# A hybrid decoder trunk on one core: x fetched back earlier, two attention tables fetched later, the convolution's LayerNorm finished one projection sooner

## The chip, the cores and the metric

One Trainium2 chip, one core of it, one program. The metric is the device time of one execution in microseconds; a program is timed several times and the median is compared. Everything is float32, with the large products made from three passes over rounded halves (below).

## What is computed

The reference is one inference step of a two-layer trunk on a prompt of 1024 tokens and a sample group of 8 sequences with 4 new tokens each. What matters here is layer 0:

```
proj = h @ e_w_in                      # 512 columns for the convolution, 2304 for q, k, v of 3 groups
glu  = a[:, :256] * sigmoid(a[:, 256:])
a    = silu(layernorm(causal depthwise conv, width 31, of glu))      # 256 channels
for grp, dilation in ((0, 1), (1, 4), (2, 16)):                      # 4 heads of 64 each
    prompt: banded attention over blocks of 128 strided tokens -> o, log sum
    sample: attention of 32 new rows over 8 caches, 129 strided keys per row
attn = mix of the 3 groups' o, weighted by their softmax denominators
x    = x + gate * (concat(a, attn) @ e_w_out)                        # then FFN, layer 1, FFN, final norm
```

## The kernel before

The residual stream `x` lies feature-major in SBUF as 8 tiles of 128 features by 1056 tokens (1024 prompt, 32 sample). `x` does not stay there during layer 0's mixer: it is stored to DRAM (`scratch_x`, 4.2 MB), its place is used by the q and k of two attention groups (`qk_fm`), and it is fetched back in two halves (`x_back`, 2112 KB each) before the down projection adds to it. The prompt attention writes its rows to DRAM as well (`scratch_o`, from the four-slot buffer `o_rows`, by ACT's DMA queue) and the three groups' tables are fetched back as `nat` (1056 KB each, `load_nat`), which are only used at `comb`, after the sample's values.

A weight unit (`w_raw`, 1 MB) is split into a high half by ACT (`split_hi`, L911) and a low half by GpSimd (`split_lo`, L1688). A projection is 16 `part`s: 2 output tiles by 8 input tiles, each 9 matmuls of 352 columns (three passes, three blocks; L1845).

All engines walk one list, `make_plan()`, and each does its share of each item, in that order; semaphores do the rest. So the list is the order on every engine. `mixed(main, fill)` spreads `fill` evenly between the steps of `main`. Attention of one group is 16 steps, each made of four items: `attend_qk` (PE makes scores of two heads, L2048; DVE adds the bias, L1452, and takes the negated maximum into `o_rows`, L1459), `attend_tr` (PE transposes the exponentials, L2056; ACT copies them to `pt`, L1071, and then makes the next step's exponentials, L936), `attend_pv` (PE, L2065; DVE copies to `o_rows`, L1463) and `attend_store` (ACT's queue sends the `o_rows` slot, L1091). The maximum of step i waits until the store of step i-4 has landed.

Small PE results go to two PSUM banks used in turn (`misc`, `misc_slot`); `attend_qk` takes both, so whatever follows it on PE that needs one waits until DVE has added the bias. Large results take two sets of three banks in turn (`big`). From the item `ring` on, during the sample's scores, there are five small banks.

The stages around the change, in order:

- group 1's projections, mixed into attention of group 0, together with 30 of the convolution's 62 taps (`conv`, DVE, L1400);
- group 2's projections v, k, q, mixed into attention of group 1: 12 taps among v's parts, then the LayerNorm's sum (`ln_sum`) early in k, its mean (`ln_mean`) between k and q, and, after q, its variance (`ln_var`);
- attention of group 2, mixed with the sample's keys: `s_kt` transposes a batch's cached keys in five pieces (PE L2086; DVE L1537 and ACT L1132 copy them to `kT`), `s_qk` multiplies them (L2097). SP fetches the keys of batch b+2 (`load_cache`, 1152 KB) when the last piece of batch b has been transposed. `ln_mid` and `sample_load` are among these items.

`ln_mean` is: PE multiplies by a matrix of constants (`mean`, L1900), DVE subtracts (L1484), ACT squares (L1106), DVE adds the squares (L1489). `ln_var` is: PE the same product, ACT Ln (L916) and Exp (L1113), DVE scales two tiles (L1496), ACT Silu on them (L1119), with an activation table load ahead of each.

## Time and profile before

| what | value |
|---|---|
| median of 3 runs | 2721.53 us (2717.16 to 2722.25) |
| the profiled execution, as timed | 2721.19 us |
| its span in the profile | 2719.4 us, 1.8 us less |
| PE busy | 2533.0 us, 93% of the span |
| DVE, ACT, GpSimd busy | 961.0, 571.4, 528.9 us |
| PE, busy share in the stretch 476 to 544 us | between 6 and 7 tenths, the lowest of the span |

The time of the profiled execution and the median differ by 0.34 us. PE is the engine to watch: where it is idle, the row's bracket says how long and what ended the idle time.

### The profile page before, as it was taken

To read this page: it belongs to the slowest core of one execution; us is meant where nothing else is said; L and a number is where in the kernel's file an instruction comes from. 1 tells how busy PE (TensorE), PEld (TensorE's weight loads), DVE (VectorE), ACT (ScalarE), POOL (GpSimd) and SP (SyncE) were. 2 spreads that over 40 slices of the span, in tenths; PEclk is the share of its full clock that TensorE was granted. 3 is DMA by queue.
4 is the path that set the end of the run, shared out by engine and by line. 5 is a ranking of instruction groups with operands and counts; after the bars stand their busy time and mean duration, and the time that the engine had idled before them with its cause. 6 is when DMAs were issued, how large, how long until landed. Compare 5 with 4: busy or idle time off the path is not lost.

```text
span 2719.4 us, 35656 instructions
## 1 busy us (share of the span) xinstructions
PE 2533.0 (93%) x16005; PEld 2411.7 (89%) x16005; DVE 961.0 (35%) x1556; ACT 571.4 (21%) x722; POOL 528.9 (19%) x175
## 2 busy tenths in 40 slices
PE   7798889688899999999999799997999999999996
PEld 4797778457899999999999799997999999999996
DVE  3465653346422222122224522436422222222226
ACT  3312223422411111111112311032311111111112
POOL 1321001100322211222112423111422211122220
PEclk8899999788999999999999899999999999999998
DMA  8112242563112221122212388310011111111101
GB/s 308 58 59 88 86 130 87 199 207 105 47 63 78 78 93 63 63 94 78 77 64 77 118 284 289 112 56 32 32 47 47 47 47 39 40 47 47 47 32 64
DMA packets 163522, 246.66 MB, mean 91 GB/s; under 512 B 5870, under 2 KB 150676, under 8 KB 162218
## 3 DMA queue, kind: packets, MB, share of 16 engines
q1 hardware_dynamic: 151078, 179.41, 20.1%
q0 software_dynamic: 3872, 60.82, 6.5%
q10 hardware_dynamic: 8420, 4.15, 0.5%
q8 instruction: 126, 2.06, 0.3%
q14 instruction: 26, 0.21, 0.0%
HBM read 225.69 MB, written 62.52 MB: 106 GB/s over the span
## 4 chain that ended last, share of the span: by engine, by line
PE 74%; DVE 3%; DMA 2%; issue 1%; ACT 1%; SPq 0%; DVEq 0%; ACTq 0%
PE ps L1845 67%; PE ps L1882 2%; PE ps L1956 1%; PE ps L1900 1%; DVE nt L1345 1%; DMA scratch_o<-o_rows 1%; DMA cache<-in_cache_b_kv 1%; DMA w_raw<-in_e_w_out 0%; PE ps L2097 0%; DVE h_lo L1371 0%; DVE nt L1354 0%; DVE tmp L1196 0%; PE ps L2086 0%; PE ps L1964 0%; DVE ln_t L1475 0%
## 5 line engine op out<-in xcount | busy, mean ns | idle before, releaser
L1688 POOL TENSOR_TENSOR w_lo<-w_raw,w_hi 128x2048 fp32r<-128x2048 f32 x93 | 435.5, 4683 | 1789.0 <-ACT w_hi L911 1789.0
L1845 PE MATMUL ps<-h_hi,w_hi 128*128 128x352 f32 x3024 | 667.8, 329 | 6.1 <-DVE h_lo L1213 3.4
L1845 PE MATMUL ps<-h_hi,w_lo 128*128 128x352 f32 x3024 | 653.6, 324 | 0.0
L1845 PE MATMUL ps<-h_lo,w_hi 128*128 128x352 f32 x3024 | 653.4, 324 | 0.0
L1845 PEld LDWEIGHTS ps<-h_hi,w_hi 128*128 128x128 f32 x3024 | 511.7, 190 | 27.0 <-issue 22.4
L1845 PEld LDWEIGHTS ps<-h_hi,w_lo 128*128 128x128 f32 x3024 | 520.7, 188 | 0.0
L1845 PEld LDWEIGHTS ps<-h_lo,w_hi 128*128 128x128 f32 x3024 | 516.2, 189 | 0.0
L1206 DVE SCALAR_TENSOR_TENSOR x<-ps,mod,x 128x704 f32<-128x704 f32 x448 | 315.5, 746 | 317.0 <-PE ps L1845 317.0
L1253 DVE TENSOR_TENSOR tmp<-ps,tmp 128x1056 f32<-128x1056 f32 x44 | 55.3, 1257 | 729.7 <-PE ps L1845 729.7
L911 ACT ACTIVATE w_hi<-w_raw 128x2048 fp32r<-128x2048 f32 x93 | 177.7, 1911 | 503.9 <-PE ps L1845 400.4
L1845 PE MATMUL ps<-mid_hi,w_hi 128*128 128x352 f32 x1248 | 274.6, 328 | 8.5 <-DVE acc_s L1207 5.2
L1845 PE MATMUL ps<-mid_hi,w_lo 128*128 128x352 f32 x1248 | 271.1, 325 | 0.0
L1845 PE MATMUL ps<-mid_lo,w_hi 128*128 128x352 f32 x1248 | 270.8, 325 | 0.0
L1845 PEld LDWEIGHTS ps<-mid_hi,w_hi 128*128 128x128 f32 x1248 | 214.3, 191 | 15.2 <-issue 6.3
L1845 PEld LDWEIGHTS ps<-mid_hi,w_lo 128*128 128x128 f32 x1248 | 216.3, 189 | 0.0
L1845 PEld LDWEIGHTS ps<-mid_lo,w_hi 128*128 128x128 f32 x1248 | 213.9, 189 | 0.0
L916 ACT ACTIVATE tmp<-ps 128x1056 f32<-128x1056 f32 x52 | 54.4, 1052 | 464.6 <-PE ps L1845 435.7
L952 ACT ACTIVATE mid_hi<-tmp 128x1056 fp32r<-128x1056 f32 x44 | 47.9, 1088 | 427.7 <-DVE tmp L1253 427.7
L1317 DVE TENSOR_TENSOR mod<-ps,vecs 128x18 f32<-128x18 f32 x48 | 8.2, 171 | 238.3 <-PE ps L1964 237.8
L1400 DVE SCALAR_TENSOR_TENSOR conv_a<-ext_p,vecs,conv_a 128x1024 f32<-128x1024 f32 x60 | 84.7, 1412 | 0.0
L1882 PE MATMUL ps<-h_hi,w_hi 128*128 128x352 f32 x192 | 43.1, 368 | 31.6 <-ACT h_hi L1028 31.6
L1882 PEld LDWEIGHTS ps<-h_hi,w_hi 128*128 128x128 f32 x192 | 37.6, 223 | 35.6 <-issue 35.6
(260 smaller groups left out, 1705.0 us busy)
## 6 DMA issues: line engine op xcount, KB each, us to landing
w_raw<-in_ada_w SPq DMA_DIRECT2D x48, 1024.0 KB, 6.6
w_raw<-in_ffn_w_gate_up SPq DMA_DIRECT2D x44, 1024.0 KB, 5.1
out_kv_sample<-in_cache_b_kv POOLq DMA_DIRECT2D x8, 4088.0 KB, 19.3
w_raw<-in_ffn_w_down SPq DMA_DIRECT2D x22, 1024.0 KB, 5.0
cache<-in_cache_b_kv SPq DMA_DIRECT2D x28, 512.0 KB, 6.2
w_raw<-in_e_w_in SPq DMA_DIRECT2D x11, 1024.0 KB, 5.7
w_raw<-in_o_w_in SPq DMA_DIRECT2D x10, 1024.0 KB, 10.2
out_kv_sample<-in_cache_b_kv POOLq DMA_DIRECT2D x8, 1016.0 KB, 6.4
```

The source lines that it names most:

```text
L911: act.activation(w_hi[u % 2], w_raw[r.slot], ACT.Copy).then_inc(w_hi_done, 1)
L916: return act.activation(blocks(dst), big(t)[:, :, 0:BLK], func, **kw).then_inc(big_free[t % 2], 1)
L952: act.activation(mid_hi[:, it.j % 2, m, :], tmp[:, m, :], ACT.Copy).then_inc(hid_hi, 1)
L1206: dve.scalar_tensor_tensor(dst, src, g, dst, ALU.mult, ALU.add)
L1253: dve.tensor_tensor(blocks(tmp[:, m, :]), T[:, :, 0:BLK], blocks(tmp[:, m, :]), ALU.mult)\
L1345: dve.scalar_tensor_tensor(nt[:, k, 0:SEQ], x[:, k, 0:SEQ], mod[:, c, k, 0:1], rs[:, 0:SEQ], ALU.mult, ALU.mult).then_inc(xn_made, 1)
L1400: ins = dve.scalar_tensor_tensor(dst, src, w, dst, ALU.mult, ALU.add)
L1688: pool.tensor_tensor(w_lo[raw_of[u].slot], w_raw[raw_of[u].slot], w_hi[u % 2].bitcast(F32), ALU.subtract)\
L1845: mm = pe.matmul(big(t)[:, b, 0:BLK], wt, xt[:, k, b * BLK:b * BLK + BLK], start=(k == 0 and n == 0), stop=(k == K - 1 and n == 2))
L1882: mm = pe.matmul(big(t + m)[:, b, 0:BLK], halves[s][:, k, m * P:m * P + P], xt[:, k, b * BLK:b * BLK + BLK], start=(k == 0 and step == 0), ...
L1900: mm = pe.matmul(big(t)[:, b, 0:BLK], mean_w, src[:, b * BLK:b * BLK + BLK], start=True, stop=True)
L1956: mm = pe.matmul(misc(it.misc)[j:j + S_TOK, 0:256], cs[:, k, :], w[:, k, :], start=(k < 4), stop=(k >= 4), skip_group_check=True)
```

## The change

Four moves in the list, and the waits that go with them; the work itself is the same.

1. Four more convolution taps (34 instead of 30) are mixed into attention of group 0; the last eight are among the first ten parts of group 2's v, with the request for group 2's bias table (`bias_in`) behind them and `ln_sum` three parts later.
2. `ln_mean` moves from between k and q to between v and k; `ln_var` from behind q to between k and q.
3. The first fetch of `x` (`x_back`, k=1) moves from the middle of group 2's attention to its beginning, and GpSimd waits with it until the keys of batch 1 have landed (`keys_landed(1)`).
4. The tables of groups 0 and 1 (`nat`) are no longer fetched at `sample_in` but when the keys of batch 2 and of batch 3 have landed.

```diff
-    mixed(attention(0), among(among(v + k + q, taps[20:50]), [ada] * 8))
+    mixed(attention(0), among(among(v + k + q, taps[20:54]), [ada] * 8))
...
-    k = k[:2] + [one("bias_in", g=2), norm_a[0]] + k[2:]
-    mixed(attention(1), among(among(v, taps[50:62]) + k + [norm_a[1]] + q, [ada] * 8))
+    v = among(v[:10], taps[54:62]) + [one("bias_in", g=2)] + v[10:13] + [norm_a[0]] + v[13:]
+    mixed(attention(1), among(v + [norm_a[1]] + k + [norm_a[2]] + q, [ada] * 8))
     ada_out()
-    norm_a[2]()
     last = attention(2)
     mixed(last[:3], [])
     items.append(Item("sample_in"))
+    items.append(Item("x_back", k=1))
+    items.append(Item("nat_in", g=0, b=2))
...
-    half = (len(last) - 3) // 2
-    mixed(last[3:15] + [one("ln_mid"), one("sample_load")] + last[15:3 + half] + [one("x_back", k=1)] + last[3 + half:], sample)
+    mixed(last[3:15] + [one("ln_mid"), one("sample_load"), one("nat_in", g=1, b=3)] + last[15:], sample)
...
+            def keys_landed(b):
+
+                slot, turn = cache_at(b)
+                pool.wait_ge(cache_loaded[slot], 48 * turn)
...
-                    load_nat(0)
-                    load_nat(1)
                 elif it.kind == "nat_in":
 
-                    pool.wait_ge(big_ready, score_item.big + 1)
-                    load_nat(2)
+                    if it.g < 2:
+                        keys_landed(it.b)
+                    else:
+                        pool.wait_ge(big_ready, score_item.big + 1)
+                    load_nat(it.g)
                 elif it.kind == "x_back":
                     if it.k:
+                        keys_landed(1)
                         pool.wait_ge(sc_max, 32)
```

On PE, at the boundary between v and k of group 2, the changed kernel has this (`tmp` is what is averaged, `sc` the exponentials; the changed kernel's lines are 7 higher, L1907 is `mean`):

```order
L1907 MATMUL ps<-tmp,mean_w 128x352 x3
L2055 MATMUL ps<-qk_fm_99 128x256 x2
L1852 MATMUL ps<-h_hi,w_hi_61 128x352 x3
L1852 MATMUL ps<-h_lo,w_hi_61 128x352 x3
L1852 MATMUL ps<-h_hi,w_lo_59 128x352 x3
L2063 MATMUL ps<-ident_sb,sc 128x128 x4
```

Before, the same stretch began with the scores: the product with `mean_w` is new there, and on DVE `ln_mean`'s two subtractions and its addition now stand ahead of the bias for these scores.

```order
L1484 SCALAR_TENSOR_TENSOR conv_a<-ps,conv_a 128x1056 x2
L1489 TENSOR_TENSOR tmp<-tmp 128x1056
L1452 TENSOR_TENSOR sc<-ps,bias 128x256 x2
L1459 TENSOR_REDUCE o_rows<-sc 128x2
L1463 COPY o_rows<-ps 128x128
```

On ACT, at the boundary between k and q, the changed kernel has `ln_var` ahead of a step's copy to `pt` and the next exponentials; before, a copy to `pt` of the same step stood there with `ln_mean`'s squares, and these rows up to the Silu came behind q:

```order
L916 ACT_TABLE_LOAD
L916 ACTIVATE tmp<-ps,vecs 128x1056
L1113 ACT_TABLE_LOAD
L1113 ACTIVATE tmp<-tmp 128x1056
L1119 ACT_TABLE_LOAD
L1119 ACTIVATE tmp<-conv_a,vecs 128x1056 x2
L1071 ACTIVATE pt<-ps 128x512
L936 ACT_TABLE_LOAD
L936 ACTIVATE sc,o_rows<-sc,o_rows 128x128 x2
```

On GpSimd's queue, at the beginning of group 2's attention (`cache_loaded0` and `cache_loaded1` are the keys' landings; L1815 is the fetch of `x`, L1713 that of a table), the changed kernel has:

```order
L1797 DMA select<-in_select 128x32
L1815 DMA x<-scratch_x 128x4224 [waits misc_free0,x_stored,sc_max,cache_loaded1]
L1713 DMA nat<-scratch_o 128x8x264 [waits o_stored2,o_stored1,o_stored3,o_stored0,cache_loaded0]
L1820 DMA kv_s<-scratch_kv 32x3x256 [waits kv_stored,mixed_ready]
L1821 DMA bias_s<-scratch_bias_s 128x480
L1713 DMA nat<-scratch_o 128x8x264 [waits o_stored2,o_stored1,o_stored3,o_stored0,cache_loaded1]
L1815 DMA x<-scratch_x 128x4224 [waits x_stored,k_stored,sc_max]
```

Before, both tables stood right behind `select`, without a wait for keys, and both fetches of `x` behind `bias_s`. SP's order is the same in both kernels.

## Rows read from the trace of the kernel before

**Rows 1.** The page: the chain that ended last, shares by engine.

```profile
PE 74%; DVE 3%; DMA 2%; issue 1%; ACT 1%; SPq 0%; DVEq 0%; ACTq 0%
```

**Rows 2.** Windows: us, busy (count) of PE, PEld, DVE, ACT, POOL, PEclk, DMA share, GB/s.

```profile
444.00:488.00 44.00, 40.36 (x281) 35.67 (x279) 10.52 (x23) 15.75 (x41) 6.55 (x2) 1.00 0.20 62
488.00:502.00 14.00, 3.59 (x19) 2.47 (x19) 7.78 (x37) 11.02 (x17) 3.47 (x5) 0.66 1.03 362
...
527.00:535.00 8.00, 1.53 (x11) 0.99 (x8) 0.74 (x2) 0.67 (x2) 0.00 (x0) 0.68 1.00 387
```

**Rows 3.** Waits of PE, 488 to 535 us: us in total, times, longest.

```profile
PE ps L2048 <- DVE sc L1452: 6.5, 1, 6.5
PE ps L2086 <- DMA cache<-in_cache_b_kv: 6.1, 1, 6.1
PE ps L2056 <- ACT sc L936: 3.4, 1, 3.4
```

**Rows 4.** Timeline behind q: start, us, engine, line, tiles, [idle before <-releaser].

```profile
486.12 2.02 PE L1900 MATMUL ps<-tmp,mean_w 128*128 128x352 f32 x6
...
488.07 0.49 PE L2048 MATMUL ps<-qk_fm 64*128 64x128 f32 x4
...
488.51 1.14 ACT L916 ACTIVATE tmp<-ps,vecs 128x1056 f32<-128x1056 f32 x1
...
492.07 2.43 DVE L1496 TENSOR_TENSOR conv_a<-conv_a,tmp 128x1056 f32<-128x1056 f32 x2 [5.60 <-ACT tmp L1113]
...
494.54 2.42 ACT L1119 ACTIVATE tmp<-conv_a,vecs 128x1056 f32<-128x1056 f32 x2 [1.20 <-DVE conv_a L1496]
...
496.98 1.28 ACT L936 ACT_TABLE_LOAD   x1
498.28 0.40 ACT L936 ACTIVATE sc<-sc,o_rows 128x128 f32<-128x128 f32 x1
...
500.46 0.80 PE L2048 MATMUL ps<-qk_fm 64*128 64x128 f32 x4 [0.56 <-ACT pt L1071]
```

**Rows 5.** Timeline, a bias addition at 426 us and the stretch of `ln_mean`.

```profile
426.08 0.42 DVE L1452 TENSOR_TENSOR sc<-ps,bias 128x256 f32<-128x256 f32 x1 [1.64 <-PE ps L2048]
...
442.88 1.94 PE L1900 MATMUL ps<-tmp,mean_w 128*128 128x352 f32 x6
...
449.41 1.26 DVE L1489 TENSOR_TENSOR tmp<-tmp 128x1056 f32<-128x1056 f32 x1 [2.13 <-ACT tmp L1106]
...
451.14 0.49 PE L2048 MATMUL ps<-qk_fm 64*128 64x128 f32 x4 [1.07 <-DVE o_rows L1463]
...
452.43 0.73 PE L1845 MATMUL ps<-h_hi,w_hi 128*128 128x352 f32 x3
```

**Rows 6.** DMA: volume, 488 to 506 us; one issue, 489.5 to 491.6 us.

```profile
DMA packets 4942, 6.51 MB, mean 362 GB/s; under 512 B 228, under 2 KB 4395, under 8 KB 4941
...
cache<-in_cache_b_kv SPq DMA_DIRECT2D x1, 512.0 KB, 11.4
```

**Rows 7.** DMA issues, 507 to 509.7 us: KB each, median us to landing.

```profile
scratch_o<-o_rows ACTq DMA_DIRECT2D x2, 33.0 KB, 2.8
```

**Rows 8.** DMA issues, 520.5 to 522.5 and 523.5 to 525 us.

```profile
x<-scratch_x POOLq DMA_DIRECT2D x1, 2112.0 KB, 12.0
...
scratch_o<-o_rows ACTq DMA_DIRECT2D x2, 33.0 KB, 9.1
```

**Rows 9.** DMA issues, 551 to 553 us.

```profile
scratch_o<-o_rows ACTq DMA_DIRECT2D x2, 33.0 KB, 4.6
```

**Rows 10.** Timeline of DVE: the maximum of steps 4, 7, 8 and 15 of group 2.

```profile
511.66 0.42 DVE L1459 TENSOR_REDUCE o_rows<-sc 128x2 f32<-128x256 f32 x1
...
534.26 0.42 DVE L1459 TENSOR_REDUCE o_rows<-sc 128x2 f32<-128x256 f32 x1 [8.18 <-DMA scratch_o<-o_rows]
...
539.05 0.42 DVE L1459 TENSOR_REDUCE o_rows<-sc 128x2 f32<-128x256 f32 x1 [0.44 <-issue]
...
570.77 0.42 DVE L1459 TENSOR_REDUCE o_rows<-sc 128x2 f32<-128x256 f32 x1
```

## Prediction

> **What bounds the kernel now.** The page's chain comes first: three quarters of it is PE's own work [rows 1], so a change that alters no work can only give back, or add, stretches in which PE stands idle or runs slowly. The list of waits then says where these lie. In the 47 us from 488 to 535 us there are three: 6.5 us for DVE's bias addition and 3.4 us for ACT's exponentials, both at the beginning of group 2's attention, and 6.1 us for a cache of keys [rows 3]. The windows show what goes with them: the granted clock is 0.66 and 0.68 there, that is partly at the lower of the two levels, 1.2 GHz, after PE had been idle, and the DMA engines are full, 1.03 and 1.00 [rows 2]. What the lower level costs a form is in two rows: the same scores take 0.49 us at 488.07 and 0.80 us at 500.46 [rows 4].
>
> The timeline shows why the first two waits exist. `ln_var`'s product ends at 488.14, ACT makes Ln and Exp, DVE scales, ACT makes the Silu until 496.96, loads a table and reaches the exponentials at 498.28 [rows 4]; attention waits behind all that on DVE and on ACT. The third has a companion: at 534.26 DVE's maximum of step 7 had waited 8.18 us for a store of `o_rows` [rows 10], whose landing took 9.1 us where it takes 2.8 without company [rows 7, 8]. The fetch of `x`, issued in the same two microseconds, took 12.0 [rows 8]. So the real chain of this stage is the store that must land before the maximum four steps on.
>
> **The change, part by part.** I count from T, the start of a `mean` product.
>
> *`ln_mean` between v and k.* Before, the addition of squares ends at 449.41 + 1.26 = 450.67, which is T + 7.8 for T = 442.88 [rows 5]. Now the scores of step 7 come right behind the product, take both small PSUM banks, and their bias addition is queued on DVE behind that addition: the first bank is free at T + 7.8 + 0.4 = T + 8.2 [rows 5]. PE has until then the product (1.5 until the next matmul can start, an estimate from its 1.94), the scores (0.7) and one part: about 1.5, since before, PE needed 451.14 - 1.07 - 442.88 = 7.2 us for a product, three parts and one `attend_pv` [rows 5]. That is 3.7. It then stands for 4.5 us at the transposes. With the product itself, this boundary costs **6.0 us**.
>
> *`ln_var` between k and q.* From the start of Ln to the end of the Silu it took 496.96 - 488.51 = 8.45 us [rows 4]. ACT copies `pt` only behind it, at about T + 10.9, and the item `tokens_new` wants that bank; PE has 7.2 + 0.4 us of work until then, so it stands 3.3 us. Then `tokens_new`, its copy off (0.7, an estimate), and the step's scores put the next part at T + 12.3, against 452.43 - 442.88 = 9.55 before, with 0.4 of transposes changing sides [rows 5]: **+2.3 us**. What is queued behind: step 12's exponentials, which have a table load of 1.28 more ahead, and the high half of a weight unit on ACT; both have a step's length to spare.
>
> At this place a page of the Trainium skill counts more: "ScalarE: Activation LUTs", section "What ACT_TABLE_LOAD costs", puts a switch at the load plus a drain of 1.38 us, 2.66 us in all. Here 496.98 + 1.28 = 498.26 and the exponential starts at 498.28 [rows 4], so there is no drain in this trace; by the page, with three switches until the Silu, the stall would be some 4 us longer and the sum 4 us later. I go by the rows.
>
> *Clock.* Two new idle stretches, 4.5 and 3.3 us, in a stage that ran at the full level, 1.00 from 444 to 488 us [rows 2]. The old ones of 9.8 and 6.1 us were followed by the lower level [rows 2, 3]. If one of 5 to 7 us of lower level follows each, at 0.80 against 0.49 per form, they cost 2 us or more each; if none, nothing. I take 2.5 together. The stage up to the end of q gets 6.0 + 2.3 + 2.5 = **10.8 us** longer; bounds 8.3 and 14.
>
> *Taps.* Four more in the earlier stage and four fewer in the later: the same DVE work, hidden behind parts of PE in both. I take 0, with 1 us either way.
>
> *Behind q.* From here I count in the old times, as if q ended at the same moment. The two waits of 6.5 and 3.4 go, and so does the product. But step 2's scores cannot be at once: the first cache must land and `q_own` be filled, for which DVE needs GpSimd's memset first. I expect them at 491.6, 8.9 before 500.46 [rows 4]. The pace behind is (570.77 - 539.05) / 7 = 4.53 us a step [rows 10], so step 4's maximum would be at 491.6 + 9.1 + 1.3 = 502.0 instead of 511.66.
>
> That is the first maximum that needs a store, and here the moved fetch of `x` counts. From 488 to 506 us 6.51 MB are moved, at 362 GB/s [rows 6]; 2.16 MB of these are the two tables, which leave, and 2.16 MB of `x` come in their place. The last piece of batch 1's keys took 11.4 us [rows 6] and landed at 500.5; without the tables' share I expect it at 494 to 495. `x` is issued then and takes up to 12.0 us [rows 8], so the engines are full until about 507, and the store of step 0, issued near 499, lands with it: 8 us, as in rows 8. Step 4's maximum comes at 507 instead of 502.0. The gain there is **4.7 us**, half of what the waits in rows 3 promise.
>
> *From step 4 to step 8.* Before: 539.05 - 511.66 = 27.4 us [rows 10]. Undisturbed: 4 x 4.53 = 18.1. `x` is gone from here, but the two tables are now fetched here, each when a cache has landed. Each is 1.06 MB, 2.9 us at the rate of rows 6. A store that meets one is late by between 1.8 (4.6 - 2.8, beside a cache load [rows 7, 9]) and 6.3 (9.1 - 2.8 [rows 7, 8]) if the maximum waits for it, by nothing otherwise. I take 2.5 each, near the lower row since a table is half of `x`. So 23.1 us, **4.3 less**. Sum of this stage -9.0; bounds: -19.0 with no store hit at all, -1.4 with both tables at 6.3.
>
> Behind step 8 nothing differs: the second half of `x`, the third table and the value caches start by the same events.
>
> **Sum.** +10.8 - 9.0 = +1.8 us on the profiled 2721.19, and 0.34 between that execution and the median: 2723.3.
>
> **The rivals.** 0.2% of the time, 5.4 us, is what a measurement here can tell from no change.
>
> *Faster.* `x` disturbs the early stores little, because step 0's store goes out before `x` is at full rate (step 4's maximum at 504, -7.7), and each table costs 1 us (-7.3); idle stretches in q's stage bring almost no lower clock (+8.8). Together -6.2: 2715.3. For it speaks that the two visible waits, 9.8 and 6.1 us [rows 3], go for sure; against it that 6.0 us at the v and k boundary follow from the order alone.
>
> *Slower.* The tables take `x`'s place as the transfer that holds the stores in the middle of the stage: both hit a store that a maximum waits for, at the 6.3 us of rows 7 and 8. The stage then gives back 1.4 only: +9.4, 2730.9. It decides from about 4.3 us for each table on. For it speaks that the maximum waits for the store that is just issued, so any transfer finds one; against it that a table is half as large as `x`. The Trainium skill says, in "DMA: Bandwidth & Descriptors", section "Queues, rings and completion order", that each DMA engine takes turns between its queues, packet by packet; by that rule a small store is slowed by how many queues are busy beside it, however much they hold, and a table would delay it as `x` does. Rows 8 and 9 leave this open, since the 4.6 us had one other queue busy and the 9.1 us two.
>
> *Nothing.* Both sides are small: no lower clock, q's stage hides most of `ln_mean` after all, and the stage behind gains little: 2721.5.
>
> **How the numbers follow.** The forecast of near cancelling has 0.46, with a range of its own of 2718 to 2728; faster 0.29, slower 0.19, nothing 0.06. From the faster case nearly all, and a little of the forecast's lower edge, lies below 2716.1: 0.29. Above 2727.0 lie most of the slower case and the forecast's upper edge: 0.23. Within: 0.48. The range 2713 to 2731 reaches to both rivals' times and leaves out what the bounds allow beyond them.
>
> **What would show it.** PE waits of about 4.5 us at the transposes behind `ln_mean` (for DVE's bias addition) and of about 3.3 us at `tokens_new` behind `ln_var` (for ACT's copy to `pt`); the clock below 1 behind them; step 4's maximum waiting for a store until the fetch of `x` has landed; no wait above 3 us for the keys of batch 3. I am wrong if PE does not wait behind `ln_mean`, if the early stores land within 5 us beside `x`, or if a store beside a table takes 8 us or more.

## The result, and the profile after

The changed kernel takes 2725.61 us in the median of 20 runs (2721.07 to 2730.98); the kernel before took 2719.04 in 20 runs beside them, 2.5 less than in the three runs that the forecast started from. The ratio is 1.0027, 95% interval 1.0020 to 1.0033, that is 7.3 us more (5.4 to 9.0). The forecast was 2723.3 with a range to 2731.0, on the side of no change; the loss is just over the bound of 0.2%. The profiled execution took 2728.81 us, 3.2 over the median, with a span of 2727.1, 7.7 us over the span before.

The chain's shares answer [rows 1]: PE's share is higher, and DMA's too, since the chain now goes through the stores of `o_rows`.

```profile
PE 77%; DVE 4%; DMA 3%; ACT 1%; issue 1%; SPq 0%; ACTq 0%; DVEq 0%
```

The windows answer [rows 2]; q now ends near 502 us, so the beginning of group 2's attention is the third row here. The stage that ran at full clock before, 444 to 488 us, is at 0.92 now.

```profile
444.00:488.00 44.00, 38.47 (x251) 33.10 (x250) 12.88 (x30) 20.48 (x40) 4.56 (x1) 0.92 0.24 79
488.00:502.00 14.00, 13.77 (x107) 12.86 (x105) 1.05 (x4) 3.84 (x11) 0.00 (x0) 1.00 0.07 20
502.00:516.00 14.00, 10.52 (x62) 8.10 (x63) 8.30 (x43) 6.64 (x25) 4.25 (x4) 0.67 0.91 298
516.00:530.00 14.00, 6.88 (x52) 3.72 (x45) 2.52 (x8) 2.90 (x8) 0.37 (x1) 0.74 0.82 281
```

The timeline of the changed kernel has the two idle stretches of PE that the order promised. At the boundary of v and k it is the wait for DVE's bias addition, 4.18 us, with the same parts of k taking 1.08 us a row behind it where they took 0.65 ahead of it; at the boundary of k and q it is the wait for ACT's copy to `pt`, 3.47, then 0.93 for DVE. These rows answer [rows 5] and [rows 4].

```profile
403.70 1.94 PE L1907 MATMUL ps<-tmp,mean_w 128*128 128x352 f32 x6
...
406.79 0.64 PE L1852 MATMUL ps<-h_lo,w_hi 128*128 128x352 f32 x3
407.27 0.64 PE L1852 MATMUL ps<-h_hi,w_lo 128*128 128x352 f32 x3
412.08 1.09 PE L2063 MATMUL ps<-ident_sb,sc 128*128 128x128 f32 x4 [4.18 <-DVE sc L1452]
412.82 1.23 PE L1852 MATMUL ps<-h_hi,w_hi 128*128 128x352 f32 x3
413.85 1.08 PE L1852 MATMUL ps<-h_lo,w_hi 128*128 128x352 f32 x3
...
465.72 0.36 PE L2035 MATMUL ps<-ident_sb,k_new 128*32 128x128 f32 x1 [3.47 <-ACT pt L1071]
...
467.65 0.80 PE L2055 MATMUL ps<-qk_fm 64*128 64x128 f32 x4 [0.93 <-DVE kv_rows L1437]
468.38 1.25 PE L1852 MATMUL ps<-h_hi,w_hi 128*128 128x352 f32 x3
```

Windows of PE alone (us, busy and count, granted clock, DMA share, GB/s) say how long the lower of the two levels, 1.2 instead of 2.4 GHz, stays behind the first of these stretches: from shortly before 412 to 418 us. Behind the second stretch it stays from 465.8 to 472.6.

```profile
408.00:410.00 2.00, 0.00 (x0) 1.00 0.11 36
410.00:412.00 2.00, 0.00 (x0) 0.79 0.00 0
412.00:414.00 2.00, 1.92 (x8) 0.50 0.04 8
414.00:416.00 2.00, 2.00 (x9) 0.50 0.00 0
416.00:418.00 2.00, 2.00 (x9) 0.51 0.00 0
418.00:420.00 2.00, 1.93 (x26) 1.00 0.00 0
```

That length is not fixed. The kernel with the LayerNorm part alone, below, has the same items here and the same wait of 4.2 us, and there the lower level lasts 3.4 us in all:

```profile
408.00:410.00 2.00, 2.00 (x9) 0.52 0.03 8
410.00:412.00 2.00, 2.00 (x10) 0.63 0.00 0
412.00:414.00 2.00, 1.93 (x25) 1.00 0.00 0
```

So it is with the tables first and with the taps early; with x in the middle it is 6.8 us as here. Behind the second stretch all five have 6.8 or 6.9 us.

Behind q, the timeline of GpSimd's queue and DVE's maxima in group 2 answer [rows 8] and [rows 10]. `x` is issued at 512.31 and takes 14.4 us; the store that the maximum of step 4 waits for goes out in two pieces, 2.2 and 2.8 us later (514.51 and 515.09), and lands with it. The three fences are the timeline, the DMA issues from 511 to 514 us, and the chain (start and length).

```profile
512.31 0.53 POOL L1815 DMA_DIRECT2D x<-scratch_x  x1 [6.48 <-DMA cache<-in_cache_b_kv]
...
527.03 0.42 DVE L1459 TENSOR_REDUCE o_rows<-sc 128x2 f32<-128x256 f32 x1 [8.24 <-DMA scratch_o<-o_rows]
...
540.78 0.42 DVE L1459 TENSOR_REDUCE o_rows<-sc 128x2 f32<-128x256 f32 x1 [3.09 <-DMA scratch_o<-o_rows]
...
551.49 0.42 DVE L1459 TENSOR_REDUCE o_rows<-sc 128x2 f32<-128x256 f32 x1 [3.69 <-DMA scratch_o<-o_rows]
```

```profile
x<-scratch_x POOLq DMA_DIRECT2D x1, 2112.0 KB, 14.4
```

```profile
515.09 11.82 DMA scratch_o<-o_rows
```

For the whole way I take marks from the timelines: the start of DVE's maximum (L1459 here) of a step, written group,step; the first product with `mean_w` behind the down projection (675.66 before, 683.05 after); and the end of the span. In us:

| stretch | before | changed | difference |
|---|---|---|---|
| start to 1,0 | 357.30 | 354.63 | -2.7 |
| 1,0 to 1,6 (v; taps) | 40.38 | 44.32 | +3.9 |
| 1,6 to 1,15 (both LayerNorm places) | 71.69 | 87.63 | +15.9 |
| 1,15 to 2,4 | 42.29 | 40.45 | -1.8 |
| 2,4 to 2,8 | 27.39 | 24.46 | -2.9 |
| 2,8 to 2,15 | 31.72 | 34.71 | +3.0 |
| 2,15 to the norm | 104.89 | 96.85 | -8.0 |
| norm to end | 2043.74 | 2044.05 | +0.3 |

The sum is +7.7, the difference of the spans. Of the first row, 1.9 us lie ahead of group 0's first maximum (211.75 before, 209.9 changed), where the two lists are the same. The marks stand a little differently to the parts of q in kernels with another number of items between the steps, so they are good to a microsecond or two, and one execution is not its median: four profiles with the same items from 1,0 to 1,15 have 129.0, 129.1, 130.7 and 131.95 us there.

### The profile page after: what moved, and what is told of

It is laid out like the page before. It is cut to its first block, busy times and chain, and to the rows that moved or that the text cites. A ratio compares the mean times of both kernels' runs of the same rounds, so it can differ in the third digit from the quotient of the medians.

```text
span 2727.1 us, 35657 instructions
## 1 busy us (share of the span) xinstructions
PE 2533.8 (93%) x16005; PEld 2413.0 (88%) x16005; DVE 960.9 (35%) x1556; ACT 571.7 (21%) x722; POOL 528.5 (19%) x175
## 4 chain that ended last, share of the span: by engine, by line
PE 77%; DVE 4%; DMA 3%; ACT 1%; issue 1%; SPq 0%; ACTq 0%; DVEq 0%
PE ps L1852 69%; PE ps L1889 2%; DMA scratch_o<-o_rows 2%; PE ps L1963 1%; PE ps L1907 1%; DVE nt L1345 1%; DMA cache<-in_cache_b_kv 1%; DMA w_raw<-in_e_w_out 0%; PE ps L1971 0%; PE ps L2104 0%; PE ps L2072 0%; DVE h_lo L1371 0%; PE ps L2055 0%; DVE nt L1354 0%; DVE tmp L1196 0%
```

## The experiments

Twelve kernels, each timed 5 to 12 times beside the kernel before; ratios are to those runs, and differences in us are these ratios times their median.

| kernel | median | before beside it | ratio, 95% interval |
|---|---|---|---|
| LayerNorm part alone | 2724.38 | 2719.53 | 1.0016, 1.0007 to 1.0025 |
| fetches alone | 2717.09 | 2719.53 | 0.9991, 0.9982 to 1.0001 |
| both products behind transposes | 2718.47 | 2719.53 | 0.9998, 0.9989 to 1.0006 |
| x in the middle | 2731.44 | 2719.53 | 1.0038, 1.0026 to 1.0051 |
| PE kept busy | 2722.70 | 2718.45 | 1.0015, 1.0004 to 1.0027 |
| taps early | 2727.77 | 2718.45 | 1.0030, 1.0019 to 1.0040 |
| tables first | 2724.66 | 2718.45 | 1.0026, 1.0011 to 1.0042 |
| behind transposes, old fetches | 2718.71 | 2718.45 | 1.0004, 0.9994 to 1.0013 |
| taps alone | 2710.65 | 2719.48 | 0.9973, 0.9961 to 0.9984 |
| taps and fetches | 2709.72 | 2719.48 | 0.9958, 0.9944 to 0.9971 |
| mean behind the scores | 2724.45 | 2717.77 | 1.0021, 1.0012 to 1.0030 |
| that, variance behind transposes, old fetches | 2719.67 | 2717.77 | 1.0010, 1.0001 to 1.0019 |

**The LayerNorm part alone.** The changed kernel's list up to q, with the fetches of before, also on GpSimd's side:

```diff
     items.append(Item("sample_in"))
-    items.append(Item("x_back", k=1))
-    items.append(Item("nat_in", g=0, b=2))
...
-    mixed(last[3:15] + [one("ln_mid"), one("sample_load"), one("nat_in", g=1, b=3)] + last[15:], sample)
+    half = (len(last) - 3) // 2
+    mixed(last[3:15] + [one("ln_mid"), one("sample_load")] + last[15:3 + half] + [one("x_back", k=1)] + last[3 + half:], sample)
...
+                    load_nat(0)
+                    load_nat(1)
...
-                        keys_landed(1)
```

> The kernel before with the first two moves alone (taps, bias request, LayerNorm steps); the fetches of x and of the two tables stand as before. Both theories: the last maximum of group 1 ends its attention 16 to 17 us later than before (469.37 to about 486), with PE idle 4.2 us at the transposes behind ln_mean and 3.5 us at tokens_new behind ln_var, each followed by about 6.7 us at a granted clock of 0.50. Theory A (these idle stretches and the half clock behind them are the loss, and the fetches change little): before + 4 to + 11 us, that is within 4 us of the changed kernel. Theory B (the LayerNorm's cost is given back behind q and the moved fetches are the loss): within 3 us of before.

Measured: 4.4 us slower than before (1.9 to 6.8), with PE waits of 4.2 and 3.5 us in the same places and 129.1 us from 1,0 to 1,15 (112.1 before, 131.95 changed). The lower clock behind the first wait lasted half as long as I expected, 3.4 us. So the greater part of the loss is there without any moved fetch. What it shows beside that: 1,15 to 2,4 took 35.3 us, 7.0 less than before and 5.1 less than in the changed kernel. The gain behind q that I forecast is there, as long as `x` is not.

**The fetches alone.** The LayerNorm and tap lines of before, the fetches of the changed kernel.

```diff
-    mixed(attention(0), among(among(v + k + q, taps[20:54]), [ada] * 8))
+    mixed(attention(0), among(among(v + k + q, taps[20:50]), [ada] * 8))
...
-    v = among(v[:10], taps[54:62]) + [one("bias_in", g=2)] + v[10:13] + [norm_a[0]] + v[13:]
-    mixed(attention(1), among(v + [norm_a[1]] + k + [norm_a[2]] + q, [ada] * 8))
+    k = k[:2] + [one("bias_in", g=2), norm_a[0]] + k[2:]
+    mixed(attention(1), among(among(v, taps[50:62]) + k + [norm_a[1]] + q, [ada] * 8))
     ada_out()
+    norm_a[2]()
```

> The kernel before with the last two moves alone: x fetched behind the keys of batch 1, the two tables behind the keys of batches 2 and 3; taps and LayerNorm as before. Both: group 1's last maximum stays at 469.4 within 1 us, and the waits of 6.5 and 3.4 us at the beginning of group 2's attention stay. Theory A: the time is that of before within 4 us, since behind q the stage swaps one transfer for another of the same size. Theory B (the moved fetches are the loss): before + 5 us or more, with a maximum of group 2 that waits 6 us or more for a store.

Measured: 2.4 us faster, which the interval does not tell from nothing (-4.9 to +0.3); 112.5 us from 1,0 to 1,15 and 42.8 to 2,4. Theory B, that the fetches are the loss, falls. (The profiled execution, 2711.79 us, is the fastest of the eleven, 5.3 under their median.) The timeline shows why an early `x` does no harm here: it is issued at 496.48 and takes 12.4 us, to 508.9. The store of step 0, which must land before step 4's maximum, goes out at 507.15, when `x` is nearly in, and lands in 2.0 us (timeline; DMA issues from 507 to 508.3 us).

```profile
496.48 0.54 POOL L1816 DMA_DIRECT2D x<-scratch_x  x1 [6.98 <-DMA cache<-in_cache_b_kv]
...
507.15 0.54 ACTq L1092 DMA_DIRECT2D scratch_o<-o_rows  x1
```

```profile
scratch_o<-o_rows ACTq DMA_DIRECT2D x2, 33.0 KB, 2.0
```

With the LayerNorm behind q the store goes out 10.7 us behind `x`; with the LayerNorm early, 2.2.

**Both products behind the transposes.** The list is cut at the two boundaries, so that each product comes behind the transposes of a step (`main[24]` and `main[44]` are the `attend_pv` behind them).

```diff
-    mixed(attention(1), among(v + [norm_a[1]] + k + [norm_a[2]] + q, [ada] * 8))
+    main = attention(1)
+    fill = among(v + [norm_a[1]] + k + [norm_a[2]] + q, [ada] * 8)
+    at = [fill.index(norm_a[1]), fill.index(norm_a[2])]
+    mixed(main[:24], fill[:at[0]])
+    norm_a[1]()
+    mixed(main[24:44], fill[at[0] + 1:at[1]])
+    norm_a[2]()
+    mixed(main[44:], fill[at[1] + 1:])
```

> The changed kernel, with ln_mean and ln_var each a few items further on, behind a step's transposes instead of behind its scores; the boundaries of v, k and q move with them. Theory A: no PE wait above 1.5 us at either place (4.2 and 3.5 before this edit), the granted clock stays at 1.00 there, and group 1's last maximum comes at 472 within 2 instead of 486.6. The kernel as a whole gains 8 to 14 us on the changed one. Rival (the part behind q is set by transfers, not by when q ends; a shorter stage is given back there): the stage gains as much, the whole under 5 us.

Measured: as fast as before (-3.0 to +1.6 us), 7.8 us under the changed kernel by the ratios. From 1,0 to 1,15 it took 121.9 us, 10 less than changed; one part of q, about 1.5 us, now comes behind the last mark and not ahead of it. PE's longest wait at the first place is 1.5 us (of the waits from 385 to 430 us, in total, times, longest):

```profile
PE ps L2062 <- DVE o_rows L1470: 1.5, 1, 1.5
```

The clock did not stay at 1.00 throughout: 0.80 from 402 to 408 us, 0.91 to 414.

The long waits are gone, but most of their time is not. From 1,0 to 1,15 (windows, length less PE's busy time) PE idles 17.2 us here, 19.9 in the changed kernel and 10.6 before; what fell is its busy time, from 112.0 to 104.6 us, with the clock at 0.96 where it was 0.91. The cut list puts every item between the steps at another place, and the idle time now lies in many waits of 2.1 us or less.

**x in the middle.** The changed kernel with `x_back` (k=1) where it stood before.

```diff
-    items.append(Item("x_back", k=1))
...
-    mixed(last[3:15] + [one("ln_mid"), one("sample_load"), one("nat_in", g=1, b=3)] + last[15:], sample)
+    half = (len(last) - 3) // 2
+    mixed(last[3:15] + [one("ln_mid"), one("sample_load"), one("nat_in", g=1, b=3)] + last[15:3 + half] + [one("x_back", k=1)] + last[3 + half:], sample)
```

> The changed kernel with the first fetch of x back in the middle of group 2's attention; tables late and LayerNorm early as changed. Theory A (x holds up the store of step 0, which took 11.8 us beside it): the first store waited for lands in 6 us or less, the maximum of step 4 comes 4 us or more sooner than 40.5 us behind group 1's last, and a store in the middle is late by 6 us in its place: the whole within 3 us of the changed kernel. Rival (the caches and the k and v stores beside it hold the store up, with or without x): the maximum of step 4 does not move by more than 1.5 us.

Measured: 1,15 to 2,4 in 32.9 us, 7.6 less than changed: `x` it was that held step 4, and the rival (caches and k and v stores alone) falls. But `x` now goes out at 530.81, 0.9 us behind the second table, and step 8's maximum pays for it; a store there took 10.55 us in the chain. 2,4 to 2,15 took 67.6 us against 59.2, and the whole is 10.3 us slower than before (7.1 to 13.9), at the upper edge of what was expected or over it. The profiled execution, 2722.96 us, is the fastest of the six and 8.5 under their median, so the trace does not hold all of that loss.

```profile
513.83 0.42 DVE L1459 TENSOR_REDUCE o_rows<-sc 128x2 f32<-128x256 f32 x1 [0.76 <-DMA scratch_o<-o_rows]
...
529.93 0.89 POOL L1713 DMA_DIRECT2D nat<-scratch_o  x1 [6.24 <-DMA cache<-in_cache_b_kv]
530.81 0.56 POOL L1815 DMA_DIRECT2D x<-scratch_x  x1
...
543.13 0.42 DVE L1459 TENSOR_REDUCE o_rows<-sc 128x2 f32<-128x256 f32 x1 [8.25 <-DMA scratch_o<-o_rows]
```

**PE kept busy.** Work whose result is overwritten fills the two idle stretches: 27 matmuls at the first part of k, 18 at that of q. Nothing is left out.

```diff
+                if m == 0 and k == 0:
+                    big_slot(it.big)
+                    for i in range({("k", 2): 9, ("q", 2): 6}.get((it.role, it.g), 0)):
+                        for b in range(3):
+                            pe.matmul(big(it.big)[:, b, 0:BLK], halves[0][:, 0, 0:P], h_hi[:, 0, b * BLK:b * BLK + BLK],
+                                      start=True, stop=True)
                 dense_tile(it.big + m, KT, lambda s, k: halves[s][:, k, m * P:m * P + P], h_hi, h_lo, k)
```

> The changed kernel with repeated work put into the two idle stretches: at the first part of group 2's k, 27 matmuls (high half by high half of that part) are made and overwritten before the part itself, and 18 at the first part of q, some 4.4 and 2.9 us of PE's time in waits of 4.2 and 3.5 us. The results are the same. Theory A (an idle stretch costs its own length and about as much again as 3.3 us in the 6.7 us at half clock behind it): the granted clock stays at 1.00 in both places, the first parts behind take 1.45 us again, not 2.6, and group 1's attention, from its first maximum to its last, takes 5 to 7 us less than the 131.95 of the changed kernel. Rival (the half clock does not come from the idle stretch, but by the run or the place): the clock falls all the same, and the stage is as long or longer.

Measured: the clock stays at 1.00 in all windows of both places, and 1,0 to 1,15 takes 126.4 us instead of 131.95, as Theory A expected, although PE does more. The transposes come without a wait, and the parts behind them are at full speed:

```profile
403.66 4.59 PE L1874 MATMUL ps<-h_hi,w_hi 128*128 128x352 f32 x27
408.09 0.64 PE L1852 MATMUL ps<-h_hi,w_hi 128*128 128x352 f32 x3
...
409.55 0.63 PE L2069 MATMUL ps<-ident_sb,sc 128*128 128x128 f32 x4
409.93 0.73 PE L1852 MATMUL ps<-h_hi,w_hi 128*128 128x352 f32 x3
410.50 0.65 PE L1852 MATMUL ps<-h_lo,w_hi 128*128 128x352 f32 x3
```

```profile
406.00:412.00 6.00, 6.00 (x41) 5.88 (x40) 2.70 (x4) 3.44 (x8) 0.00 (x0) 1.00 0.00 0
412.00:418.00 6.00, 5.25 (x46) 4.33 (x45) 1.38 (x5) 1.98 (x2) 4.25 (x1) 1.00 0.29 83
```

So the lower clock behind the two stretches cost up to 5.6 us in the changed kernel. Counted from 1,6, since the filling stands behind it, it is 82.4 us against 87.6; three other profiles with the same items have 86.3 to 87.1. The price is thus 4.0 to 5.3 us. The whole: 4.1 us over before (1.1 to 7.3), against 7.3; the direction fits, the two intervals overlap.

**Taps early.** The last eight taps also go into group 0's stage; empty items keep everything else in place.

```diff
-    mixed(attention(0), among(among(v + k + q, taps[20:54]), [ada] * 8))
+    mixed(attention(0), among(among(v + k + q, taps[20:62]), [ada] * 8))
...
-    v = among(v[:10], taps[54:62]) + [one("bias_in", g=2)] + v[10:13] + [norm_a[0]] + v[13:]
+    v = among(v[:10], [lambda: None] * 8) + [one("bias_in", g=2)] + v[10:13] + [norm_a[0]] + v[13:]
```

> The changed kernel with its last eight convolution taps moved too, from among group 2's v into attention of group 0 (42 taps there); everything else keeps its place. Theory A (eight taps among ten parts hold up the scores of steps 3 to 6, 3 us by the trace): the way from group 1's first maximum to that of step 6 takes 40.4 within 1 us as in the kernel before, not 44.3, and attention of group 0 gets longer by under 1 us: the whole 3 us under the changed kernel. Rival (the vector engine is as full in group 0's stage): group 0's stage gets longer by 2 to 4 us and nothing is won.

Measured: both halves of both theories. 1,0 to 1,6 takes 38.4 us instead of 44.3, so the eight taps did hold up those steps, by 4.2 to 5.9 us against the four profiles that have them at the same places (42.6 to 44.3). But group 0's attention, from its first maximum to its last, takes 131.5 us (125.6 changed), with a PE wait of 6.5 us there, and the whole is 8.2 us over before (5.2 to 10.9). In this profile 42 taps there cost more than they save, and the rival is right too.

```profile
PE ps L2028 <- DVE sc L1452: 6.5, 1, 6.5
```

**Tables first.** The changed kernel, with the tables of groups 0 and 1 at the beginning again.

```diff
-    items.append(Item("nat_in", g=0, b=2))
...
-    mixed(last[3:15] + [one("ln_mid"), one("sample_load"), one("nat_in", g=1, b=3)] + last[15:], sample)
+    mixed(last[3:15] + [one("ln_mid"), one("sample_load")] + last[15:], sample)
...
+                    load_nat(0)
+                    load_nat(1)
                 elif it.kind == "nat_in":
...
```

> The changed kernel with the tables of groups 0 and 1 fetched at the beginning again, as before, but x still behind the keys of batch 1. Theory A (what holds the stores is whatever large transfer is under way, so the order only moves the loss): 4.3 MB stand together at the beginning, the maximum of step 4 comes 40 to 45 us behind group 1's last (40.5 with the tables late), and step 4 to step 15 takes 53 to 56 us (59.2 with them late): the whole within 3 us of the changed kernel. Rival (a late table costs a store at every place where it meets one, an early one nothing): the whole 4 us or more under the changed kernel.

Measured: 38.9 us from 1,15 to 2,4 and 55.6 from there to 2,15 (40.5 and 59.2 in the changed kernel), as expected except that step 4 lost nothing by the tables; 7.1 us over before (3.0 to 11.4), so the same as the changed kernel as far as twelve runs between 2716 and 2737 us can tell. The rival, 4 us or more under the changed kernel, is not borne out, but the interval just reaches it.

**Behind the transposes, old fetches.** The cut list of the third run with the fetches of the first; no further edit.

> The LayerNorm steps behind the transposes, as in the run of that name, with all fetches as before. Theory A (with q ending without idle stretches, the early x costs step 4 some 7 us, as the kernel with the LayerNorm part alone showed: 35.3 us from group 1's last maximum to step 4's, and not 40.5): 33 to 36 us here, against 41.3 with x early, the maximum of step 15 at 94 to 96 us behind group 1's last against 99.5, and the whole 3 to 6 us under the 2718.5 of that run, so under both kernels. Rival (the values' stage is set by transfers that start at fixed places and gives any gain back): step 15 earlier by as much, the whole within 2 us of 2718.5.

Measured: 37.6 us to 2,4 (41.3 with `x` early) and 96.8 to 2,15 (99.5), about half of the gain that I expected; the whole, 1.1 us over before (-1.6 to +3.5), is not under that run. Here the rival is the nearer one. PE idles 17.2 us from 1,0 to 1,15 here too.

**Taps alone, taps and fetches.** After eight kernels one thing stood out: with 34 taps, group 0's attention took 119.8 to 122.4 us in six profiles (125.6 in that of the changed kernel), with 30 taps 125.7 and 126.0. So the tap move was tried by itself, and with the fetches.

```diff
-    mixed(attention(0), among(among(v + k + q, taps[20:50]), [ada] * 8))
+    mixed(attention(0), among(among(v + k + q, taps[20:54]), [ada] * 8))
...
-    mixed(attention(1), among(among(v, taps[50:62]) + k + [norm_a[1]] + q, [ada] * 8))
+    mixed(attention(1), among(among(v, taps[54:62]) + k + [norm_a[1]] + q, [ada] * 8))
```

> The kernel before with one thing changed: 34 convolution taps in attention of group 0 instead of 30, and 8 instead of 12 among group 2's v. LayerNorm and fetches as before. Theory (with 34 taps in this arrangement five of six kernels ran attention of group 0, first to last maximum, in 119.8 to 122.4 us at a granted clock of 0.99, against 125.7 and 126.0 with 30 taps at 0.93; the idle stretches there stay too short or too scattered for the clock to fall): 120 to 123 us here, with group 1's stage at 112 within 1.5, and the whole 3 to 6 us under before. Rival (the granted clock there falls or not by chance, whatever the taps): 125 us or more in this profile, or the whole within 2 us of before.

> The same with the moved fetches too (x behind the keys of batch 1, the two tables behind those of batches 2 and 3); only the LayerNorm stays as before. Theory: the gains add, 3 to 6 us from the taps and 2.4 from the fetches, so 5 to 8 us under before, the fastest version of this study. Rival (a gain ahead of the values' stage is given back there): within 2 us of the kernel with the moved fetches alone, 2.4 us under before.

Measured: taps alone are 7.3 us faster than before (4.4 to 10.6), taps and fetches 11.4 (7.9 to 15.2), the fastest kernel here and faster than both that were compared. In the profile of the taps alone, group 0's attention took 122.3 us, 3.8 less, and group 1's 110.0, 2.1 less. In that of taps and fetches group 0's took 126.5, so the size of that part is not firm: over the eleven profiles with 34 taps, two of them the runs below, it is 122.7 in the mean, and the clock there between 0.92 and 0.99. In group 1 one cause can be read off. With fewer items between the steps, `ln_mean`'s product now comes right behind the scores of step 12 and ahead of the transposes. The bias addition of these scores is ahead of its DVE work, so that the transposes follow without a wait, and the next scores, which waited 1.07 us for a DVE copy before [rows 5], don't wait either:

```profile
434.07 0.49 PE L2048 MATMUL ps<-qk_fm 64*128 64x128 f32 x4
434.49 2.04 PE L1900 MATMUL ps<-tmp,mean_w 128*128 128x352 f32 x6
...
435.54 0.48 DVE L1452 TENSOR_TENSOR sc<-ps,bias 128x128 f32<-128x128 f32 x2
...
437.05 2.41 DVE L1484 SCALAR_TENSOR_TENSOR conv_a<-ps,conv_a 128x1056 f32<-128x1056 f32 x2
...
437.81 0.60 PE L2056 MATMUL ps<-ident_sb,sc 128*128 128x128 f32 x4
...
441.59 1.26 DVE L1489 TENSOR_TENSOR tmp<-tmp 128x1056 f32<-128x1056 f32 x1 [2.13 <-ACT tmp L1106]
```

**Mean behind the scores.** That order, put into the changed kernel: only `ln_mean` moves, past one `attend_qk` (`main[23]` is the transposes).

```diff
-    mixed(attention(1), among(v + [norm_a[1]] + k + [norm_a[2]] + q, [ada] * 8))
+    main = attention(1)
+    fill = among(v + [norm_a[1]] + k + [norm_a[2]] + q, [ada] * 8)
+    at = fill.index(norm_a[1])
+    mixed(main[:23], fill[:at])
+    norm_a[1]()
+    mixed(main[23:], fill[at + 1:])
```

> The changed kernel with ln_mean one step's item further on: the scores of step 7 now stand ahead of its product, so that their bias addition is queued on DVE ahead of ln_mean's subtractions and addition. All else as changed. Theory (the idle stretch of 4.2 us comes from that queue order alone, and the half clock from the stretch): no PE wait above 1.5 us there, the granted clock stays at 1.00 until ln_var, the way from the first maximum of group 1 to the last is 5 to 7 us shorter than 131.95, and the whole 4 to 7 us under the changed kernel, 0 to 3 us above before. Rival (the small banks are taken by the next scores instead, and the wait only moves): a wait of 3 us or more at the next transposes or scores, and the whole within 2 us of the changed kernel.

Measured: the wait of 4.2 us is gone, the longest from 385 to 440 us is 1.1, the clock is 1.00 from there until `ln_var`, and 1,0 to 1,15 takes 126.8 us, 5.2 less. 1,6 to 1,8, where the edit is, takes 19.4 instead of 24.9. Elsewhere in the stage other waits are longer: in total PE idles 18.8 us from 1,0 to 1,15, only 1.1 less than in the changed kernel. In the whole it shows much less too: 5.7 us over before (3.3 to 8.2), against 7.3. The local theory holds; that the whole would follow it does not, at least within these intervals.

**The last one.** The same cut at `main[23]` for the mean, at `main[44]` for the variance, old fetches.

> ln_mean behind the scores as in the run of that name, ln_var behind the transposes, all fetches as in the kernel before. Theory: with neither idle stretch and without an early x, group 1's attention takes 118 to 121 us and step 15 of group 2 comes 94 to 97 us behind it; the whole 2 to 5 us under 2718.7, the same with ln_mean behind the transposes. Rival (that kernel's remaining loss is the vector engine's load among the ten first parts, not ln_mean's place): within 1.5 us of 2718.7. Either way it is expected above the 2709.7 of the kernel with the moved taps and fetches and the LayerNorm left alone.

Measured: 124.5 us for group 1's attention, 97.5 from 1,15 to 2,15; the whole 2.7 us over before (0.3 to 5.2), no better than with the mean behind the transposes, as its rival said. PE idles 19.5 us in the stage, as much as in the changed kernel. 1,0 to 1,6 still takes 43.5 us, with a PE wait of 3.7 us for DVE's copy to `o_rows`; with the mean behind the scores it is 3.5. The timelines show what these copies stand behind. In each kernel with taps between 1,0 and 1,6, one tap runs on DVE beside GpSimd's `split_lo` of 4.6 us and takes 3.5 to 4.3 us instead of 1.28. In these two kernels a second tap is queued between that one and the copy; with the mean behind the transposes none is, and the waits for this copy are 0.3 and 0.5 us.

## Why the prediction was near, and where its steps were wrong

*`ln_mean` between v and k, +6.0.* Right. The idle stretch was 4.18 us for 4.5, at the transposes and for the bias addition, as derived from the order; moving the product past one item takes it away.

*`ln_var` between k and q, +2.3.* Right as well. The idle stretch was 3.47 us for 3.3, at `tokens_new`, for ACT's copy. I missed 0.93 us behind it, when the next scores wait for DVE's copy of `kv_rows`. The rule of the Trainium skill that I set against my rows ("ScalarE: Activation LUTs", "What ACT_TABLE_LOAD costs") would have made this stretch some 4 us longer, by an estimate from its 1.38 us a switch. The trace after again shows no drain: the copy ends at 465.57, the load of 1.28 us starts at 465.59, and the exponentials start at 466.88.

*Clock, +2.5.* Right in kind, too small in size. I had bound it by "2 us or more each; if none, nothing" and took 2.5 for both. Each stretch is followed by 6.8 us at 0.50 in the changed kernel, and the run that kept PE busy puts 4.0 to 5.3 us on both together. How long the lower level lasts behind the same wait differs, 3.4 or 6.8 us, so a single number was not to be had.

*Taps, 0 within 1.* Wrong in both directions. I looked at the work, which is the same, and not at its place in DVE's queue. Steps 0 to 6 of group 1 take 2.2 to 3.9 us longer in the four profiles with these eight taps, and 4.2 to 5.9 go when the taps do. It is not their number for each part, which hardly changes: 8 in 10 against 12 in 16. In the changed kernel PE waits 2.4 and 1.5 us there for DVE's copy to `o_rows`, queued behind a tap each time (2.0 us in all before), and the granted clock is 0.88 instead of 0.96. The move of four taps into group 0's stage, which I had taken to be neutral as well, is worth 7.3 us by itself when the rest stays spread, though it too shifts the places of other items.

Of the 19.9 us that group 1's attention got longer, the parts are then 4.2 + 3.5 + 0.9 of idle time, 1.9 for `ln_var`'s product, 4.0 to 5.3 of clock and 3.9 about the taps: 18.4 to 19.7, less the 1.1 that PE waited behind `ln_mean` before [rows 5]. I had 10.8. The windows agree: PE's idle time grew by 9.3 us (10.6 to 19.9) and its busy time by 10.5 (101.5 to 112.0), 1.9 of it the product and most of the rest the lower clock, that among the taps included. The same items took 129.1 us in the kernel with the LayerNorm part alone, so some 3 us of the 19.9 belong to the execution.

*Behind q, step 4, -4.7.* The mechanism was right and is shown: without an early `x`, step 4 comes 5.1 us sooner (LayerNorm part alone) or 7.6 (x in the middle). The size was off: the store took 11.8 us where I took 8, since `x` took 14.4, and the gain was 1.8.

*Step 4 to 8, -4.3.* Measured -2.9; the waits for stores beside the tables were 3.1 and 3.7 us. These two stores took 5.7 and 6.0 us to land (chain, 534.98 and 545.02), but the next three, beside keys alone, took 5.0, 6.1 and 4.5, so a share of the tables' own is not shown. (A table of 1056 KB is 1.08 MB and not the 1.06 of the prediction, which changes nothing.)

*"Behind step 8 nothing differs."* Wrong. 3.0 us are lost until step 15, in waits for stores of 2.3, 3.4, 1.2 and 1.3 us, and 8.0 are given back from there to the norm. Over all fourteen profiles that stretch takes between 96.2 and 105.5 us, and the clock over its first 75 us goes along with it: 104.9 us at 0.84 before, 96.8 at 0.95 after, 96.2 at 0.95 with x in the middle, 102.5 at 0.86 with PE kept busy. Waits for the value caches are in it too, so a later start might wait less; but the windows of the two traces (before, then changed) leave the 8 us to the clock.

```profile
570.77:675.66 104.89, 87.30 (x595) 74.53 (x593) 60.36 (x110) 22.97 (x31) 10.48 (x4) 0.86 0.49 164
586.20:683.05 96.85, 78.83 (x586) 68.10 (x586) 60.26 (x110) 22.71 (x30) 10.54 (x4) 0.95 0.53 177
```

PE idles 17.6 us of the one and 18.0 of the other; its busy time is 8.5 us less. Why the clock is higher there in the changed kernel stays open.

So the forecast of +1.8 against +7.3 came near by luck. The stage with the LayerNorm was 9.1 us worse than its sum, the way from there to step 8 4.3 worse and that to step 15 3.0 worse; against them, the part behind step 15, for which I had given no reason to change, was 8.0 better, and the start 2.7.

*The rivals.* "Both tables hit a store" is not what made it slower. With the tables first, the kernel takes as long within its interval, and the slow outcome came from the stage with the LayerNorm. The rule of the Trainium skill that stood behind that rival ("DMA: Bandwidth & Descriptors", "Queues, rings and completion order"), as I had applied it, had a table delay a store as much as `x` does. The trace does not agree with that: the stores took 5.7 and 6.0 us beside a table and 11.8 beside `x` (9.1 before [rows 8]), so more than the number of queues counts.

*How the parts add.* Taps -7.3, taps and fetches -11.4, all with the LayerNorm +7.3: the early LayerNorm, with the taps placed as it needs them, costs 18.7 us. With the old fetches it costs 4.4 + 7.3 = 11.7. The difference is of the size of what the store behind `x` takes back (5.1 us at step 4), but the intervals, 3 us each way, leave room. Of these 11.7 us the kernel without the two long waits (behind the transposes, old fetches) takes back 3.3. The other 8.4 go with PE's idle time in the stage, 17.2 us against 8.1 with the taps alone, in short waits that no run takes apart. Seen so, the change held one gain that is clear, a second that its interval does not separate from nothing, and a loss larger than both.

## What to carry to other kernels

Ask of a moved chain of small steps what is queued behind it on each in-order engine: here one item's difference, the scores ahead of the product or behind it, decides about 5 us of the stage. Count a new idle stretch of TensorE like these two at its length and, where the clock falls behind it, at about half more (4.0 to 5.3 us beside 8.6 idle here). Give work that is "only moved" a price for what it then stands ahead of in its queue. Look at the idle time of the whole stage and not at the longest wait: here two long waits went, and 17.2 to 19.5 of 19.9 us stayed. Before moving several things at once, time each alone: the best kernel here is the change without its main part.

## What was new about the hardware

An idle stretch of 4.2 us on PE, at the same place in the list, was followed by 6.8 us at a granted clock of 0.50 in two kernels and by 3.4 us in three. Matmuls whose result is thrown away, 4.6 us of them in the same place, kept it at 1.00 and made the stage 4.0 to 5.3 us shorter for two such places. The same stage runs at 0.92 in one kernel and at 0.99 in another with the same items there (group 0's attention, 126.5 and 119.8 us). A DVE tap that runs beside a GpSimd `split_lo` of 4.6 us took 4.2 us in the changed kernel, where others take 1.28. A store of 33 KB took 2.0 us issued 10.7 us behind a fetch of 2.1 MB that was then nearly in, and 11.8 issued 2.8 us behind one.
